# Attention heads in pairs: the score and value matmuls of two heads issued together in the second block's mixer

## The reference

```
def hybrid_mixer(x, w_in, ...):
    qa, ka, va, qkv_b, beta_raw, dt_raw, z, gate_raw = split(x @ w_in)
    ya = sliding_window_attention(qa, ka, va, pos_bias, sink) @ w_branch_a
    qkv_b = silu(causal_depthwise_conv(qkv_b, conv_w))
    ...                      # gated delta rule on qkv_b, times silu(z)
    return (gate_a * ya + gate_b * yb) @ w_out

# one query block of the attention, per head
s = q @ k.T * 64 ** -0.5 + bias          # 128 x 128 for block 0, 128 x 256 for block 1
m = max(s.max(-1), sink)
p = exp(s - m); p = p / (p.sum(-1) + exp(sink - m))
o = p @ v
```

## Time and profile before

| | |
|---|---|
| median of the runs | 2641.73 us |
| span of the profiled execution | 2640.4 us |
| PE busy | 2375.5 us, 90% of the span |
| DVE busy | 1675.4 us, 63% |
| ACT busy | 1117.3 us, 42% |
| POOL busy | 498.6 us, 19% |
| chain that ended last | PE 73%, DVE 21%, ACT 3% |
| first scores and last value matmuls of the first mixer | 1118.9 and 1258.4 us |
| the same of the second mixer | 2003.1 and 2142.5 us |

### The profile page before, as it was taken

How to read it: one execution, slowest core, us unless ns; L and a number is a source line. 1 busy time by engine, 2 the same in 40 slices (tenths; PEclk the granted TensorE clock), 3 DMA queues, 4 the chain that set the end, 5 groups by cost and what they waited for, 6 DMA issues and landing times.

```text
span 2640.4 us, 37438 instructions
## 1 busy us (share of the span) xinstructions
PE 2375.5 (90%) x15755; PEld 2143.8 (81%) x15755; DVE 1675.4 (63%) x1946; ACT 1117.3 (42%) x1452; POOL 498.6 (19%) x379
## 2 busy tenths in 40 slices
PE   4879997886999899899899889999989899889998
PEld 4668887764898899888698789989988778788997
DVE  6977765798655644599544564464467964447544
ACT  2334433665444444455333344343445553234343
POOL 2112113332200200345022020020032522112000
PEclk9889998888899899999898999999999998898999
DMA  9768873223455456545221155555564442013652
GB/s 321 250 210 275 291 244 93 84 76 103 163 188 176 161 187 180 163 129 138 67 65 49 66 174 190 178 172 179 191 142 152 127 115 64 23 59 128 209 186 101
DMA packets 304282, 400.47 MB, mean 152 GB/s; under 512 B 43215, under 2 KB 262969, under 8 KB 304116
## 3 DMA queue, kind: packets, MB, share of 16 engines
q1 hardware_dynamic: 283360, 336.75, 40.2%
q0 software_dynamic: 17504, 57.89, 6.9%
q10 hardware_dynamic: 3252, 3.45, 0.4%
HBM read 393.86 MB, written 4.19 MB: 151 GB/s over the span
## 4 chain that ended last, share of the span: by engine, by line
PE 73%; DVE 21%; ACT 3%; issue 2%; DMA 1%; POOL 0%; SPq 0%; ACTq 0%; DVEq 0%; POOLq 0%
PE tiles L490 14%; PE tiles L491 14%; PE tiles L492 14%; PE y_rows L490 6%; PE y_rows L491 6%; PE y_rows L492 6%; DVE conv_qkv_t L1609 3%; DVE weights_lo L1289 3%; PE tiles L845 2%; PE tiles L859 2%; PE tiles L855 1%; PE tiles L829 1%; DVE xt_lo L1382 1%; DVE ada_acc L1339 1%; DVE rnn_conv_out L1548 1%
## 5 line engine op out<-in xcount | busy, mean ns | idle before, releaser
L1289 DVE TENSOR_TENSOR weights_lo<-weights_raw,weights_hi 128x2048 fp32r<-128x2048 f32 (+2 forms) x316 | 740.2, 2347 | 530.3 <-ACT weights_hi L948 529.9
L490 PE MATMUL tiles<-xt_hi,weights_hi 128*128 128x256 f32 (+1 forms) x3216 | 930.4, 289 | 33.0 <-DVE xt_lo L1382 24.5
L491 PE MATMUL tiles<-xt_lo,weights_hi 128*128 128x256 f32 (+1 forms) x3216 | 921.2, 286 | 0.0
L492 PE MATMUL tiles<-xt_hi,weights_lo 128*128 128x256 f32 (+1 forms) x3216 | 920.3, 286 | 0.0
L948 ACT ACTIVATE weights_hi<-weights_raw 128x2048 fp32r<-128x2048 f32 (+2 forms) x316 | 593.0, 1880 | 218.6 <-PE y_rows L492 191.2
L490 PEld LDWEIGHTS tiles<-xt_hi,weights_hi 128*128 128x128 f32 (+1 forms) x3216 | 621.7, 193 | 52.0 <-issue 38.2
L491 PEld LDWEIGHTS tiles<-xt_lo,weights_hi 128*128 128x128 f32 (+1 forms) x3216 | 622.0, 193 | 3.3
L492 PEld LDWEIGHTS tiles<-xt_hi,weights_lo 128*128 128x128 f32 (+1 forms) x3216 | 621.1, 193 | 0.0
L490 PE MATMUL y_rows<-weights_hi,hid_hi 128*128 128x512 f32 x608 | 244.0, 401 | 0.0
L491 PE MATMUL y_rows<-weights_lo,hid_hi 128*128 128x512 f32 x608 | 242.7, 399 | 0.0
L492 PE MATMUL y_rows<-weights_hi,hid_lo 128*128 128x512 f32 x608 | 242.5, 399 | 0.0
(11 more groups left out here) (334 smaller groups left out, 3320.5 us busy)
## 6 DMA issues: line engine op xcount, KB each, us to landing
weights_raw<-in_ffn_w_dram SPq DMA_DIRECT2D x132, 1024.0 KB, 5.1
weights_raw<-in_mlp_w_dram SPq DMA_DIRECT2D x64, 1024.0 KB, 5.8
weights_raw<-in_w_in_dram SPq DMA_DIRECT2D x52, 1024.0 KB, 5.4
ada_ring<-in_ada_w_dram POOLq DMA_DIRECT2D x76, 512.0 KB, 4.9
weights_raw<-in_rnn_w_in_dram SPq DMA_DIRECT2D x16, 768.0 KB, 4.8
ada_ring<-in_ada_w_dram SPq DMA_DIRECT2D x20, 512.0 KB, 7.7
weights_raw<-in_w_in_dram SPq DMA_DIRECT2D x32, 256.0 KB, 4.4
weights_raw<-in_w_branch_a_dram SPq DMA_DIRECT2D x32, 256.0 KB, 4.6
```

The lines of the kernel that those rows point to most:

```text
L490: pe.matmul(o, a, c, start=first, stop=False)
L491: pe.matmul(o, a, d, start=False, stop=False)
L492: return pe.matmul(o, b, c, start=False, stop=last)
L1289: dve.tensor_tensor(slot_view(WLO, m, NSPL), slot_view(RAW, m, NRAW), slot_view(WHI, m, NSPL).bitcast(F32), ALU.subtract).then_inc(*inc("l ...
```

## The change

`scores` now takes a pair t (heads 2t and 2t+1) and opens two PSUM tiles. It issues the 128x128 score matmuls of both heads, then the 128x256 ones. `mix` takes a pair too, and alternates between the heads at each of its three matmuls. Both are issued in even rounds only. Odd rounds have the slot and `turn` alone. Heads 2t and 2t+1 lie in different halves of the array's rows (scores) or columns (mix). Since the pair needs both heads' `PTA` buffers, ACT must wait in even rounds for the pair's `mix` before it copies the next head's transposed probabilities.

```
-                def scores(j):
-                    t, hh = divmod(j, 2)
...
+                def scores(t):
+                    if t == 0:
                         pe.wait_ge(*past("free_A", (s, "ka", 0)))
...
+                    banks = [topen((s, "sc", 2 * t + hh), "D") for hh in range(2)]
+                    for hh in range(2):
+                        lo, hi = 64 * hh, 64 * hh + 64
+                        pe.matmul(banks[hh][:, 0:P], QA[lo:hi, t, 0:P], KA[lo:hi, t // 4, 0:P], start=True, stop=True)
+                    for hh in range(2):
+                        lo, hi = 64 * hh, 64 * hh + 64
+                        ins = pe.matmul(banks[hh][:, P:384], QA[lo:hi, t, P:S], KA[lo:hi, t // 4, :], start=True, stop=True)
+                        ins.then_inc(*inc("tile_done", (s, "sc", 2 * t + hh)))
...
+                def mix(t):
+                    pe.wait_ge(*past("free_A", (s, "pt", 2 * t + 1)))
+                    pe.wait_ge(*past(*(("free_D", (s, "oa", t - 2)) if t >= 2 else ("y_free", (s - 1, 1)))))
+                    bank = y_bank(2 + t % 2)
+                    for q in range(3):
+                        for hh in range(2):
+                            kv = 2 * (t // 4) + hh
+                            o = bank[64 * hh:64 * hh + 64]
+                            v = VA[:, :, kv * 64:(kv + 1) * 64]
+                            pt = PTA[:, hh, :]
+                            ins = pe.matmul(o[:, P * (q > 0):P * (q > 0) + P], v[:, q // 2, :], pt[:, q * P:(q + 1) * P],
+                                            start=(q < 2), stop=(q != 1))
+                    ins.then_inc(*inc("tile_done", (s, "oa", t)))
...
-                    if j < 16:
-                        scores(j)
+                    if j < 16 and j % 2 == 0:
+                        scores(j // 2)
                     if 2 <= j < 18:
                         turn(j - 2)
-                    if j >= 3:
-                        mix(j - 3)
+                    if j >= 4 and j % 2 == 0:
+                        mix((j - 4) // 2)
...
                         act.wait_ge(*past("tile_done", (s, "pt", j - 2)))
+                        if j >= 4:
+                            act.wait_ge(*past("tile_done", (s, "oa", j // 2 - 2)))
                         evac((s, "pt", j - 2), PTA[:, j % 2, :], src=y_bank(j % 2)[:, 0:384])
```

22 lines of the change are left out of this document (removed).

## The result

The changed kernel takes 2663.18 us (median of 4 runs, 2659.08 to 2663.7) against 2641.93 (4 runs, 2641.48 to 2643.64). The ratio is 1.0073, with a 95% interval of 1.0061 to 1.0085: slower by 21 us. I had forecast 2647.1 with a range up to 2652.5. The sign I gave the larger chance to was right, though only by 0.45 against 0.44 for no change. The size was off by a factor of four, and the time lies outside the range. The profiled execution took 2663.19 us with a span of 2661.4, at a mean granted clock of 0.922; the span before was 2640.4 at 0.935. In every execution the time is 1.8 us above the span, so the span of before is not, as I wrote, the time of its execution. The forecast stands on the median and isn't changed by it.

What follows compares the result with a forecast made beforehand. DVE was taken to bound rounds 1 to 11, PE round 12's transposes to round 15's scores. Terms summed to +2.68 us per mixer, twice +5.4, on 2641.7 giving 2647.1 us; range 2638 to 2652.5.

Steps and rivals of the forecast that it cites:

- (a): Round 0: the second head's scores stand before slot 1 and delay DVE; +0.43 us per mixer (bounds -0.1 and +0.54).
- (b): Rounds 1 to 11: DVE's list is unchanged and only the phase of POOL's product shifts; 0 us.
- (c): Round 11: POOL's product falls beside the normalisation that round 12's transposes wait for; +1.0 us per mixer (bounds 0 and 1.0).
- one of my signs: The prediction would be wrong if the DVE rounds changed in length; no size given.
- Rival 4: Even rounds 4 to 12: POOL's product avoids the normalisation, saving 10.5 us in both mixers, 2636.6 us; chance 0.07.
- (d): Round 12's transposes to slot 15's end, on PE: saved switches and middle overlap give -0.75 us per mixer (bounds -0.1, -2.0).
- rival 1: Paired scores and values: full overlap of the two heads, +0.1 us per mixer, about 2641.9 us; chance 0.23.
- (e): Head 14's transposes to the `ba` slot: last pair waits for ACT's copies; +0.90 us per mixer (bounds +0.16, +1.44).
- (f): Round 15's end: PE idles about 4.1 us, so the clock may halve behind it; +1.1 us per mixer (bounds 0, +1.6).

Runs made afterwards that it cites:

- e3: The changed kernel with extra matmuls, results overwritten, ahead of the transposes PE waits for, so that PE doesn't idle there; 2656.49 us, ratio 1.0058.
- r4: e3 with 5 (first mixer) and 10 (second) extra unused matmuls ahead of round 0, to start attention later; 2656.23 us, ratio 1.005.
- h1: The kernel before with paired heads only where PE is the bound, rounds 0 to 11 left as they were; 2648.52 us, ratio 1.0015.
- r1: The kernel before with 5 and 10 unused matmuls ahead of round 0 (first, second mixer) and PE's waits filled with useless matmuls; 2658.92 us, ratio 1.0062.

## Why the prediction was wrong, step by step

**(a) and (b), rounds 0 to 11**: forecast +0.43. Up to the transposes of round 12, changed work and POOL together cost 3.2 us per mixer, and (c) holds 2.3 of it. The overlap made the pair of scores in round 0 free. In the even rounds L1600 takes 1.55 to 1.63 us as expected. From round 4 on the convolution behind it takes 3.73 to 3.75, not the 2.7 that I had read from before, but the low part keeps its 2.28, so again it comes to nothing in sum. The rounds did grow a little, by 0.9 us in all up to round 12 beside (c); that they would not was one of my signs. Rival 4, in which POOL's product goes where it does no harm, did not come.

**(c), round 11's normalisation beside POOL**: forecast +1.0 with 1.0 as the upper bound. The collision came, but with both of POOL's products: +0.80 on L1600 and +1.53 on L1633 (1.76 against 0.23). I had priced only the normalisation, and set the bound from one row, though the trace of before has L1632 at 1.35 us (1231.14, shown above). The clock has little part in it: with 7 us at half clock (e3) the transposes of round 12 still come at 111.82 us, with none (r4) at 112.20.

**(d), to the end of slot 15**: forecast -0.75 with half overlap. Overlap was complete, so by my own sum it should have been -2.0, as rival 1 has it, and h1 shows just that (21.3 us instead of 23.3). Here it was 1255.48 - 1231.57 = 23.9 us against 23.3: +0.6. The missing 2.6 us are the half clock from 1230.66 to 1237.49, behind the 3.08 us wait of (c).

**(e), the end**: forecast +0.90. That the transposes start 4.44 us behind the slot came true within 0.02, and the wait for ACT's copy is in the record with 0.58 us. From the transposes to the slot it was 5.26 instead of 3.20, +2.1; at full clock rival 1's +0.16 would be due, so some 1.9 us belong to (f).

**(f), the clock**: this is the step that failed. I took it as one row: one wait, one span of half clock behind it, +1.1 us, and upper bound 1.6. The runs put in its place: 38 us at half clock in the stretch instead of 7, in rounds 2, 4, 6, 8, 12 and at the end, where I had one place; and a later part longer by 2.9 us without a changed instruction, for which my sum had no term. e3 and r4 show the size. With the clock kept up, the change costs +0.7 us per mixer (1.4 by e3). My steps (a) to (e) with full overlap sum to -0.1 + 1.0 - 2.0 + 0.16 = -0.9. The difference is in (c), whose second instruction I left out: r4 against r1 has +2.4 up to round 12 and -1.7 behind it, where full overlap gives +0.9 and -1.8. The other 9 or so of the 10.1 us per mixer come with the clock: some 6 of them in the attention stretch, where filling PE's waits takes them away, and the 2.9 of the later part by its place, where the clock as the cause is likely but not shown.

**What I could have seen.** The earlier trace rows showed half clock behind one wait of 3.05 us, and the page the mean of 0.935. The kernel before had only 7 us of half clock in 147 us, though PE waited for DVE in nine rounds. That was a place on the grid that happened to suit it (at all five other places tried, the unchanged order took 149.3 to 154.5 us), and it should have counted as a risk on one side: this change or eight useless matmuls could lose it. That the place matters, the trace of before alone did not show. The chance for "slower" should have been higher, and the range should have reached some 20 us up.

**What stays open.** Why places 1.5 to 1.6 suit the stretch and 1.8 does not, and why the later part has a step between 1.70 and 1.71, is described by the tables, not derived. Whether the change's mean cost over places (1.5 us) differs from its cost at full clock (0.7 to 1.4) four places can't tell. The later part was never run with its waits filled.

## What to carry to other kernels

Before an edit to a kernel in which PE waits often for a microsecond or more, sum the time at half clock by stretch. Where it is low in spite of many waits, a shift may lose it (here all five other places did), so give the range its room. Judge such an edit by a stretch with the waits filled or at several starting offsets, not by one median: here 1 us of added work per mixer cost one kernel 19 us, and 2 us of it bought another 4. Pairs of matmuls on different halves of the array paid here where PE is the bound (2.0 us in the z slots of h1) and nowhere else. The greater gain was to put work that is due anyway into PE's waits.

## What the runs showed of the hardware that was not expected

- Two fp32 products on the two row halves (scores) or the two column halves (values) of the array run wholly at the same time: 0.86 us for two heads against 0.85 for one, and 0.80 against 0.80. In serial order within the pair, the values take 1.08 and the scores still 0.86.
- A DVE instruction on 128 x 2 elements took 1.76 us beside a POOL product (1.35 in the kernel before), against 0.23 alone. Its small size did not protect it.
- Changes of the granted clock stand on one grid of times for the whole run. The same 977 matmuls of an attention stretch took 146.8 to 154.5 us by their place on it, and the same later part 230.1 to 236.7; parts of different kernels that start at one place agree within 0.2 us.
- The same program ahead leads to the same place: first scores of the first mixer at 1.48 to 1.53 us behind the grid in all 11 traces without added work ahead of them.
